# Attention scores in two key halves, and a head spread moved up to stand directly behind them

## The chip, the core and the metric

The kernel runs as one program on one core of a Trainium2 chip. The metric is the device time of one execution in microseconds (us), lower is better. Matrix products run on TensorE (PE in the profile), elementwise work and reductions on VectorE (DVE), exponentials, square roots and copies on ScalarE (ACT), the subtraction that splits the weights on GpSimd (POOL); SyncE (SP) issues the loads of the weights.

## The reference, cut to what matters

Two transformer blocks run one after the other on 512 tokens of width 1024. The change touches three attentions with heads of 64 channels. In the first block that is a causal attention with a bias by distance ("moba" in the kernel). In the even layer of the second block two attentions stand side by side: one over a window of 128 tokens to either side with a sink, and one over a neighbourhood of a grid.

```python
qa = _rmsnorm(qa.reshape(B, S, A_KV_HEADS, A_GROUP, HEAD_DIM), qn_a)
ka = _rmsnorm(ka.reshape(B, S, A_KV_HEADS, HEAD_DIM), kn_a)
oa = _window_gqa(qa, ka, va, sink_a)
qb = _rmsnorm(qb.reshape(B, S, B_HEADS, HEAD_DIM), qn_b)
kb = _rmsnorm(kb.reshape(B, S, B_HEADS, HEAD_DIM), kn_b)
ob = _neighbourhood_attn(qb, kb, vb, rpb_b)
return jnp.concatenate([oa, ob], axis=-1) @ w_out
```

Queries and keys of every head are normalised over their 64 channels (`_rmsnorm`) before the scores. In each attention the score of a query and a key is their product over 64 channels in full float32; bias and mask follow, then a softmax over the keys, then the product with the values.

## The kernel before, in words

Everything is kept feature-major: a block is 128 channels on the partitions and 512 tokens along the free axis. A large product is split into three (high weights with high inputs, high with low, low with high), all of 512 columns; one "unit" is a block of 128 output channels, 8 such triples. The weights come in a ring of four units (`RING`): SP loads a unit, ACT rounds it to its high part, POOL subtracts to get the low part, PE multiplies.

Each engine has its own program, written out by hand in program order, with semaphores between the engines. `pair_attention` (on PE from line 850, on ACT from line 1595, on DVE from line 2277) works through items. An item is one pair of heads and one tile of 128 queries, with 128 to 512 keys. The two heads lie on partitions 0 to 63 and 64 to 127, so each of their score products uses 64 rows of the array; the scores of the two heads go into two banks of `score_ps`. One item goes through these steps:

- PE `scores` (L858): one product for each head over all keys of the item.
- DVE `logits` (L2286): adds the bias and finds the maximum, which frees `score_ps` (semaphore `scores_used`).
- ACT `exps` (L1604, L1607), then DVE `divide` (L2295 to L2299).
- PE `turned` (L867) transposes the probabilities into `turn_ps`, ACT `copies` (L1615) brings them back.
- PE `values` (L882) multiplies by the values into `out_ps`.

The PE loop is skewed: step i holds the scores of item i, the values of item i-3, the transposes of item i-2, and at its end a hook `between(i)` in which the caller places other work. It is a strict order: a wait in the hook holds back all that stands behind it on PE.

The window attention has 16 items, so 19 steps (0 to 18) on PE. Its hook `prepare_neighbour` (L1338 on PE) prepares the neighbour attention beside it. `WINDOW_PIECES` places pieces of the projections (`piece`, L621 to L623). `WINDOW_TURNS` places transposes of values at steps 9, 13 and 17 (L1332). Steps 1 to 8 sum squares per head (L657). Step 10 transposes the norm factors of all 8 blocks into rows (`turn_head_columns`, L664). Then ACT takes the high part of these rows (`high_rows`, L1694) and DVE the low part (`low_rows`, L2178, semaphore `rows_ready`). Steps 11 to 18 each spread one block's factors over its channels (`neighbour_spread`, which is `head_spread`, L670): one product of 64 rows with 512 columns into `gemm_ps[:, 0, :]`. DVE then scales the block by it (`head_scaled`, L2090, semaphore `spread_used`). The first spread waits for `rows_ready`, each later one for `spread_used` of the one before. The neighbour attention follows, with the same helper.

Of the kernel before, what the change touches and what calls it, by code (L numbers as in the profile page):

```python
# [30 lines left out]
P = 128  # L31
# [5 lines left out]
HD = 64  # L37
# [147 lines left out]
def build(nc, x_in, mem_in, w_in, par_in, con_in, moba_in, alibi_in, na_in, dist_in, out):  # L185
    with ExitStack() as ctx:
# [8 lines left out]
        score_ps = ctx.enter_context(nc.psum_tensor("score_ps", [P, 2, N], F32))  # L195
# [133 lines left out]
        def pair_items(kind):  # L329

            items = []
            for b in range(2 if kind == "moba" else 4):
                for t in range(T):
                    lo, hi = (0, t + 1) if kind == "moba" else (max(t - 1, 0), min(t + 2, T))
                    qs, ks = slice(t * P, (t + 1) * P), slice(lo * P, hi * P)
                    it = dict(nk=(hi - lo) * P, tile=t, group=b, last=t == T - 1, first=t == 0, turned=False, sink=None)
                    heads = [slice((2 * b + s) * HD, (2 * b + s + 1) * HD) for s in range(2)]
                    if kind == "moba":
                        it.update(q=proj1[:, A_Q + b, qs], k=proj1[:, A_K + b, ks], to=4 + b,
                                  bias=[moba_bias[:, 2 * b + s, (3 - t) * P:4 * P] for s in range(2)],  # L340
                                  v=[[values_moba[:, c, r] for c in range(lo, hi)] for r in heads])
                    elif kind == "window":
                        it.update(q=proj2[:, E_AQ + b, qs], k=proj2[:, E_AK, ks], to=b,
                                  bias=[alibi[:, 2 * b + s, (lo - t + 1) * P:(hi - t + 1) * P] for s in range(2)],
                                  sink=par[:, PCOL["sink"] + 2 * b:PCOL["sink"] + 2 * b + 2],
                                  v=[[values_a[:, c, s * HD:(s + 1) * HD] for c in range(lo, hi)] for s in range(2)])
                    else:
                        it.update(q=proj2[:, E_BQ + b, qs], k=proj2[:, E_BK + b, ks], to=4 + b, turned=True,
                                  bias=[na_bias[t][:, 2 * b + s, :] for s in range(2)],
                                  v=[[values_b[:, c, r] for c in range(lo, hi)] for r in heads])  # L350
                    items.append(it)
            return items

        def pair_probs(i, s, nk, wide):

            a = (2 * (i % 3) + s) * (N if wide else 3 * P)
            return y_all[:, a:a + nk]
# [211 lines left out]
        def _(pe):  # L569
# [47 lines left out]
            def piece(n, o, first, end, h, l):  # L617

                for kt in range(first, end):
                    w = slice(kt * P, (kt + 1) * P)  # L620
                    pe.matmul(o, wh[:, n % RING, w], h[:, kt, :], start=(kt == 0), stop=False)  # L621
                    pe.matmul(o, wh[:, n % RING, w], l[:, kt, :], start=False, stop=False)
                    m = pe.matmul(o, wl[:, n % RING, w], h[:, kt, :], start=False, stop=(kt == KT - 1))  # L623
                if end == KT:
                    m.then_inc(unit_done, 1)
# [34 lines left out]
            def turn_head_columns(bank):  # L660

                take(head_columns_ready)
                for c in range(T):
                    m = pe.transpose(bank[0:HEAD_ROWS, c * P:(c + 1) * P],  # L664
                                     head_columns[:, c * HEAD_ROWS:(c + 1) * HEAD_ROWS], ident)
                m.then_inc(head_columns_turned, 1)
# [180 lines left out]
                crossed(1, 3, 4).then_inc(unit_done, 1)  # L847
                taken[group_used] = groups0 + 4

            def pair_attention(items, between=lambda i: None, wide=False):  # L850
                groups0 = taken.get(group_used, 0)

                def scores(i, it):
                    if i:
                        take(scores_used)
                    for s in range(2):
                        r = slice(s * HD, (s + 1) * HD)
                        m = pe.matmul(score_ps[:, s, 0:it["nk"]], it["q"][r, :], it["k"][r, :], start=True, stop=True)  # L858
                    m.then_inc(scores_ready, 1)

                def turned(i, it):
                    take(probs_ready)
                    for s in range(2):
                        a = pair_probs(i, s, it["nk"], wide)
                        for c in range(it["nk"] // P):
                            t = slice(c * P, (c + 1) * P)
                            m = pe.transpose(turn_ps[:, s, t], a[:, t], ident)  # L867
                    m.then_inc(probs_turned, 1)

                def values(i, it):  # L870
                    if it["first"] and groups0 + it["group"] >= 2:
                        pe.wait_ge(group_used, groups0 + it["group"] - 1)
                    chunks = it["nk"] // P
                    for c in range(chunks):
                        for s in range(2):
                            o = out_ps[s * HD:(s + 1) * HD, it["group"] % 2, :]
                            if it["turned"]:
                                q = P // 8
                                o = o.rearrange("p (r c) -> p c r", r=8)[:, it["tile"] * q:(it["tile"] + 1) * q, :]
                            else:  # L880
                                o = o[:, it["tile"] * P:(it["tile"] + 1) * P]
                            m = pe.matmul(o, it["v"][s][c], pair_turned[i % 2][:, s, c * P:(c + 1) * P],  # L882
                                          start=(c == 0), stop=(c == chunks - 1))
                    m.then_inc(item_done, 1)

                n = len(items)
                for i in range(n + 3):
                    if i < n:
                        scores(i, items[i])
                    if i >= 3:  # L890
                        take(probs_copied)
                        values(i - 3, items[i - 3])
                    if 2 <= i < n + 2:
                        turned(i - 2, items[i - 2])
                    between(i)
                take(scores_used)
                taken[exp_ready] = taken.get(exp_ready, 0) + n
                taken[group_used] = groups0 + items[-1]["group"] + 1
# [387 lines left out]
            def query_spread(b, bank):  # L1286

                head_spread(b, QUERY_ROWS, bank)
# [14 lines left out]
            for t in range(T):  # L1303
                m = pe.transpose(turn_ps[:, 0, t * P:(t + 1) * P], proj2[:, E_AV, t * P:(t + 1) * P], ident)
# [15 lines left out]
            def neighbour_stat(b):  # L1320

                head_stat(b, y[:, 7 + b % 2, :], gemm_ps[:, 0, :])

            def neighbour_spread(b):

                head_spread(b, NEIGHBOUR_ROWS, gemm_ps[:, 0, :])
# [8 lines left out]
            def prepare_neighbour(i):  # L1335
                if i == 1:
                    take(copied_v)
                    take(spread_used)  # L1338
                if 1 <= i <= 8:
                    neighbour_stat(i - 1)  # L1340
                if i in WINDOW_PIECES:
                    u, first, end = WINDOW_PIECES[i]
                    if first == 0:
                        pe.wait_ge(unit_split, even + u + 1)
                        pe.wait_ge(emptied, even + (7 if u == 8 else u))
                        if u > 14:
                            take(copied_v)
                    piece(even + u, gemm_ps[:, 1, :], first, end, xh, xl)
                if i == 0:
                    pe.wait_ge(emptied, even + 8)  # L1350
                    query_spread(3, gemm_ps[:, 0, :])
                if i in WINDOW_TURNS:
                    turn_neighbour(WINDOW_TURNS[i])
                if i == 10:
                    turn_head_columns(gemm_ps[:, 0, :])
                if i == 11:
                    take(rows_ready)
                if 11 < i <= 18:
                    take(spread_used)
                if 11 <= i <= 18:  # L1360
                    neighbour_spread(SPREAD_ORDER[i - 11])
            pair_attention(pair_items("window"), prepare_neighbour)
            outputs0 = taken[group_used]

            def window_part(i):
# [31 lines left out]
            for kt in range(KT):  # L1397
                m = pe.matmul(o, wl[:, n % RING, kt * P:(kt + 1) * P], xh[:, kt, :], start=False, stop=(kt == KT - 1))
# [1564 lines left out]
```

## Time and profile before

| what | value |
|---|---|
| runs before (3) | 2170.11, 2170.78 and 2171.26 us, median 2170.78 us |
| profiled execution, first to last instruction (span) | 2169.7 us |
| median of the runs less that span | 1.08 us |
| PE busy | 2149.4 us, 99% of the span, 10303 instructions |
| DVE, ACT, POOL busy | 983.0, 847.1 and 893.9 us |
| HBM traffic | 88 GB/s over the span |

The page gives the profiled execution's time as its span; the 1.08 us are what lies around it in a timed run. Busy times are shares over very different stages, and a record of PE includes the depth of the pipeline, so the spacing of starts in the timeline says more than the mean of a record. A float32 product stands in the trace as two records.

### The profile page before, as it was taken

The numbers are of one execution on the slowest core, as the hardware profiler recorded it, in microseconds if no ns is written. First come the engines' busy times: TensorE is split into PE (matmuls) and PEld (weight loads), VectorE is DVE, ScalarE is ACT, GpSimd is POOL, SyncE is SP. The second block draws the span as 40 slices with busy tenths as digits, with TensorE's granted clock in tenths as the row PEclk, the third lists the DMA queues.
The fourth block names the chain that finished last, engine by engine and source line by source line (L and its number), as shares of the span: only waits on it lengthen the run. The fifth ranks groups of instructions, "written<-read, shape, count | busy, mean of one in ns | idle before, by whom it ended". The sixth has DMA issues, their size and how long they took to land.

```text
span 2169.7 us, 27420 instructions
## 1 busy us (share of the span) xinstructions
PE 2149.4 (99%) x10303; PEld 1731.4 (80%) x10303; DVE 983.0 (45%) x1496; ACT 847.1 (39%) x1282; POOL 893.9 (41%) x684
## 2 busy tenths in 40 slices
PE   9999999999999999999999999999999999999999
PEld 7875787788888877767888888888888878888887
DVE  5755645576626143465432231346534655313221
ACT  6435645422222243565433232444333434423221
POOL 5431254154444443213444444433343315444443
PEclk9999999999999999999999999999999999999999
DMA  4222132133322332102222222322222213222223
GB/s 175 78 68 69 57 99 78 59 102 122 106 97 97 110 113 88 50 30 69 97 97 97 97 97 97 106 81 75 78 87 78 72 44 109 97 97 97 97 97 97
DMA packets 55109, 193.24 MB, mean 89 GB/s; under 512 B 6112, under 2 KB 6368, under 8 KB 54752
## 3 DMA queue, kind: packets, MB, share of 16 engines
q1 hardware_dynamic: 50112, 180.41, 25.0%
q10 hardware_dynamic: 4896, 11.41, 1.6%
q8 instruction: 73, 1.20, 0.2%
q14 instruction: 28, 0.23, 0.0%
HBM read 189.69 MB, written 2.10 MB: 88 GB/s over the span
## 4 chain that ended last, share of the span: by engine, by line
issue 52%; POOL 29%; PE 17%; POOLq 1%; DMA 0%; DVE 0%; ACT 0%; SPq 0%; ACTq 0%
POOL wl L552 29%; PE gemm_ps L587 6%; PE gemm_ps L588 6%; PE gemm_ps L589 6%; POOLq L549 0%; POOLq L561 0%; DMA x<-x_in 0%; DVE xl L2090 0%; ACT xh L1892 0%; ACT wh L1497 0%; PE turn_ps L729 0%; DVE x L2236 0%; SPq L526 0%; ACTq L1891 0%
## 5 line engine op out<-in xcount | busy, mean ns | idle before, releaser
L552 POOL TENSOR_TENSOR wl<-raw,wh 128x512 fp32r<-128x512 f32 x678 | 890.1, 1335 | 1258.0 <-ACT wh L1497 1248.8
L1497 ACT ACTIVATE wh<-raw 128x1024 fp32r<-128x1024 f32 x339 | 358.7, 1059 | 752.7 <-DMA raw<-w_in 742.1
L587 PE MATMUL gemm_ps<-xh,wh 128*128 128x512 f32 x1176 | 465.8, 396 | 0.0
L589 PE MATMUL gemm_ps<-xh,wl 128*128 128x512 f32 x1176 | 459.0, 390 | 0.0
L588 PE MATMUL gemm_ps<-xl,wh 128*128 128x512 f32 x1176 | 458.8, 390 | 0.0
L588 PE MATMUL gemm_ps<-arena_r,wh 128*128 128x512 f32 (+1 forms) x1088 | 417.0, 383 | 0.0
L587 PE MATMUL gemm_ps<-arena_r,wh 128*128 128x512 f32 (+1 forms) x832 | 320.0, 385 | 1.2 <-POOL wl L552 0.7
L589 PE MATMUL gemm_ps<-arena_r,wl 128*128 128x512 f32 (+1 forms) x832 | 317.4, 381 | 0.0
L587 PEld LDWEIGHTS gemm_ps<-xh,wh 128*128 128x128 f32 x1176 | 221.5, 188 | 49.6 <-issue 2.3
L588 PEld LDWEIGHTS gemm_ps<-xl,wh 128*128 128x128 f32 x1176 | 221.5, 188 | 47.4 <-issue 2.2
L589 PEld LDWEIGHTS gemm_ps<-xh,wl 128*128 128x128 f32 x1176 | 221.3, 188 | 46.7
L588 PEld LDWEIGHTS gemm_ps<-arena_r,wh 128*128 128x128 f32 x1088 | 205.0, 188 | 41.2 <-issue 1.4
L2090 DVE SCALAR_TENSOR_TENSOR arena<-gemm_ps,rstd 128x512 f32<-128x512 f32 (+1 forms) x116 | 84.7, 731 | 261.9 <-PE gemm_ps L589 211.1
L2236 DVE TENSOR_TENSOR x<-x,gemm_ps 128x512 f32<-128x512 f32 x84 | 57.6, 686 | 316.8 <-PE gemm_ps L589 305.1
L587 PEld LDWEIGHTS gemm_ps<-arena_r,wh 128*128 128x128 f32 x832 | 157.0, 189 | 33.7 <-issue 2.4
L589 PEld LDWEIGHTS gemm_ps<-arena_r,wl 128*128 128x128 f32 x832 | 156.9, 189 | 30.1
L2097 DVE SCALAR_TENSOR_TENSOR tmp<-gemm_ps,rstd 128x512 f32<-128x512 f32 x64 | 44.2, 691 | 207.9 <-PE gemm_ps L589 207.9
L587 PE MATMUL gemm_ps<-y_r,wh 128*128 128x512 f32 x256 | 100.0, 391 | 0.0
L589 PE MATMUL gemm_ps<-y_r,wl 128*128 128x512 f32 x256 | 99.6, 389 | 0.0
L2586 DVE TENSOR_TENSOR arena_r<-sq,arena_r 128x512 fp32r<-128x512 f32 x64 | 93.7, 1464 | 2.2
L621 PE MATMUL gemm_ps<-xh,wh 128*128 128x512 f32 x216 | 88.5, 410 | 1.3 <-DVE xl L2308 0.5
L623 PE MATMUL gemm_ps<-xh,wl 128*128 128x512 f32 x216 | 84.6, 392 | 0.0
(429 smaller groups left out, 2548.6 us busy)
## 6 DMA issues: line engine op xcount, KB each, us to landing
raw<-w_in SPq DMA_DIRECT2D x338, 512.0 KB, 3.4
arena<-na_in ACTq DMA_DIRECT2D x14, 256.0 KB, 2.7
out<-x ACTq DMA_DIRECT2D x8, 256.0 KB, 2.9
x<-x_in SPq DMA_DIRECT2D x6, 256.0 KB, 6.5
arena<-alibi_in ACTq DMA_DIRECT2D x6, 256.0 KB, 3.5
arena<-moba_in ACTq DMA_DIRECT2D x1, 1024.0 KB, 4.8
arena<-mem_in ACTq DMA_DIRECT2D x1, 1024.0 KB, 5.6
arena<-dist_in ACTq DMA_DIRECT2D x1, 896.0 KB, 4.5
```

The lines of the kernel that those rows point to most:

```text
L552: m = pool.tensor_tensor(wl[:, k, half], raw[:, k, half], wh[:, k, half].bitcast(F32), ALU.subtract)
L587: pe.matmul(o, wh[:, n % RING, w], h[:, kt, 0:width], start=(kt == 0), stop=False)
L588: pe.matmul(o, wh[:, n % RING, w], l[:, kt, 0:width], start=False, stop=False)
L589: last = pe.matmul(o, wl[:, n % RING, w], h[:, kt, 0:width], start=False, stop=(kt == nkt - 1))
L621: pe.matmul(o, wh[:, n % RING, w], h[:, kt, :], start=(kt == 0), stop=False)
L623: m = pe.matmul(o, wl[:, n % RING, w], h[:, kt, :], start=False, stop=(kt == KT - 1))
L1497: act.activation(wh[:, k % RING, :], raw[:, k % RING, :], ACT.Copy).then_inc(high_split, 1)
L2090: sent(dve.scalar_tensor_tensor(out=o, in0=a, scalar=scalar, in1=b, op0=op0, op1=op1), s)
L2097: done(dve.scalar_tensor_tensor(out=o, in0=a, scalar=scalar, in1=b, op0=op0, op1=op1), s)
L2236: sent(dve.tensor_tensor(x[:, e, :], x[:, e, :], bank(n0, e), ALU.add), emptied)
L2586: done(dve.tensor_tensor(l[:, b, :], sq[:, b % 2, :], h[:, b, :].bitcast(F32), ALU.subtract), rhs_ready)
```

## The change

Two things change, on PE alone. First, `scores` cuts the keys of an item that has more than 128 of them into two halves and issues head 0 and head 1 of the first half, then head 0 and head 1 of the second. Second, `pair_attention` gets a second hook, `behind_scores(i)`, directly after the scores of step i; the waits and the spread of steps 11 to 18 move from `prepare_neighbour` into it. All three callers (moba, window, neighbour) get the halves, the window call alone the new hook.

```diff
-            def pair_attention(items, between=lambda i: None, wide=False):
+            def pair_attention(items, between=lambda i: None, wide=False, behind_scores=lambda i: None):
                 groups0 = taken.get(group_used, 0)
 
                 def scores(i, it):
                     if i:
                         take(scores_used)
-                    for s in range(2):
-                        r = slice(s * HD, (s + 1) * HD)
-                        m = pe.matmul(score_ps[:, s, 0:it["nk"]], it["q"][r, :], it["k"][r, :], start=True, stop=True)
+                    part = it["nk"] // 2 if it["nk"] > P else P
+                    for k0 in range(0, it["nk"], part):
+                        ks = slice(k0, k0 + part)
+                        for s in range(2):
+                            r = slice(s * HD, (s + 1) * HD)
+                            m = pe.matmul(score_ps[:, s, ks], it["q"][r, :], it["k"][r, ks], start=True, stop=True)
                     m.then_inc(scores_ready, 1)
...
                     if i < n:
                         scores(i, items[i])
+                    behind_scores(i)
                     if i >= 3:
                         take(probs_copied)
                         values(i - 3, items[i - 3])
...
                 if i == 10:
                     turn_head_columns(gemm_ps[:, 0, :])
+
+            def spread_neighbour(i):
                 if i == 11:
                     take(rows_ready)
                 if 11 < i <= 18:
                     take(spread_used)
                 if 11 <= i <= 18:
                     neighbour_spread(SPREAD_ORDER[i - 11])
-            pair_attention(pair_items("window"), prepare_neighbour)
+            pair_attention(pair_items("window"), prepare_neighbour, behind_scores=spread_neighbour)
```

The place on which most rests is PE's program at step 11 of the window attention, from the transposes of the norm factors (`head_columns`) at the end of step 10. `y_r,pair_r` is the first spread. Before, with the nine products of the piece between the last two groups:

```order
L664 MATMUL gemm_ps<-con,head_columns 32x128 x3
L858 MATMUL score_ps<-arena 128x256 [waits scores_used]
L858 MATMUL score_ps<-arena 128x256
L882 MATMUL out_ps<-tmp,arena 64x128 [waits group_used,probs_copied]
L882 MATMUL out_ps<-tmp,arena 64x128 x3
L867 MATMUL turn_ps<-con,y_all 128x128 [waits probs_ready]
L867 MATMUL turn_ps<-con,y_all 128x128 x5
...
L670 MATMUL gemm_ps<-y_r,pair_r 128x512 [waits rows_ready]
L858 MATMUL score_ps<-arena 128x256 [waits scores_used]
```

And now:

```order
L664 MATMUL gemm_ps<-con,head_columns 32x128 x3
L861 MATMUL score_ps<-arena 128x128 [waits scores_used]
L861 MATMUL score_ps<-arena 128x128 x3
L670 MATMUL gemm_ps<-y_r,pair_r 128x512 [waits rows_ready]
L885 MATMUL out_ps<-tmp,arena 64x128 [waits group_used,probs_copied]
L885 MATMUL out_ps<-tmp,arena 64x128 x3
L870 MATMUL turn_ps<-con,y_all 128x128 [waits probs_ready]
L870 MATMUL turn_ps<-con,y_all 128x128 x5
```

The spread and its wait for the factor rows moved up past 4 value products, 6 transposes and the nine products of the piece, and the two score products of 256 columns became four of 128.

The second place is PE's steps 13 and 14, where no piece stands at the end of step 13 but four transposes of values (L1332 before, L1336 now). Before:

```order
L670 MATMUL gemm_ps<-y_r,pair_r 128x512 [waits spread_used]
L858 MATMUL score_ps<-arena 128x384 [waits scores_used]
L858 MATMUL score_ps<-arena 128x384
L882 MATMUL out_ps<-tmp,arena 64x128 [waits probs_copied]
L882 MATMUL out_ps<-tmp,arena 64x128 x5
L867 MATMUL turn_ps<-con,y_all 128x128 [waits probs_ready]
L867 MATMUL turn_ps<-con,y_all 128x128 x3
L1332 MATMUL gemm_ps<-con,arena 128x128 [waits emptied]
L1332 MATMUL gemm_ps<-con,arena 128x128 x3
L670 MATMUL gemm_ps<-y_r,pair_r 128x512 [waits spread_used]
```

And now:

```order
L861 MATMUL score_ps<-arena 128x192 [waits scores_used]
L861 MATMUL score_ps<-arena 128x192 x3
L670 MATMUL gemm_ps<-y_r,pair_r 128x512 [waits spread_used]
L885 MATMUL out_ps<-tmp,arena 64x128 [waits probs_copied]
L885 MATMUL out_ps<-tmp,arena 64x128 x5
L870 MATMUL turn_ps<-con,y_all 128x128 [waits probs_ready]
L870 MATMUL turn_ps<-con,y_all 128x128 x3
L1336 MATMUL gemm_ps<-con,arena 128x128 [waits emptied]
L1336 MATMUL gemm_ps<-con,arena 128x128 x3
L861 MATMUL score_ps<-arena 128x192 [waits scores_used]
```

A spread stood ahead of the scores of the next step and stands behind the scores of its own step now; it still touches a score product on one side.

## Rows read from the trace of the kernel before

**Rows 1.** The page: busy time by engine, share of the span, instructions.

```profile
PE 2149.4 (99%) x10303; PEld 1731.4 (80%) x10303; DVE 983.0 (45%) x1496; ACT 847.1 (39%) x1282; POOL 893.9 (41%) x684
```

**Rows 2.** Timeline of PE, steps 9 to 12: start, length, idle before and releaser.

```profile
909.71 0.92 PE L858 MATMUL score_ps<-arena 64*128 64x384 f32 x4
910.56 0.66 PE L882 MATMUL out_ps<-sq,arena 128*64 128x128 f32 x8
...
914.83 0.70 PE L858 MATMUL score_ps<-arena 64*128 64x256 f32 x4
915.46 0.66 PE L882 MATMUL out_ps<-tmp,arena 128*64 128x128 f32 x8
...
919.31 0.50 PE L670 MATMUL gemm_ps<-y_r,pair_r 64*128 64x512 f32 x1 [0.30 <-DVE y_r L2178]
920.24 0.70 PE L858 MATMUL score_ps<-arena 64*128 64x256 f32 x4 [0.43 <-DVE small L2286]
```

**Rows 3.** Timeline of ACT, then of DVE, up to the factor rows and behind them.

```profile
917.98 0.57 ACT L1694 ACTIVATE y_r<-gemm_ps 32x512 fp32r<-32x512 f32 x1
918.58 0.68 DVE L2178 TENSOR_TENSOR y_r<-gemm_ps,y_r 32x512 fp32r<-32x512 f32 x1 [4.35 <-ACT y_r L1694]
919.29 0.48 DVE L2286 CUSTOM_DVE_ANT_0 y_all<-score_ps,arena,par 128x256 f32<-128x256 f32 x1
921.16 0.74 DVE L2090 SCALAR_TENSOR_TENSOR arena<-arena,par,gemm_ps 128x512 f32<-128x512 f32 x1
```

**Rows 4.** Timeline of PE, steps 13 and 15: a spread beside scores, and one alone.

```profile
923.89 1.13 PE L858 MATMUL score_ps<-arena 64*128 64x384 f32 x4
924.95 0.88 PE L882 MATMUL out_ps<-tmp,arena 128*64 128x128 f32 x12
...
926.78 0.49 PE L670 MATMUL gemm_ps<-y_r,pair_r 64*128 64x512 f32 x1
...
935.82 0.50 PE L670 MATMUL gemm_ps<-y_r,pair_r 64*128 64x512 f32 x1
936.25 0.88 PE L882 MATMUL out_ps<-sq,arena 128*64 128x128 f32 x12
```

**Rows 5.** Timeline of PE: sixteen score records of 128 columns, heads in turn (L1085).

```profile
84.42 1.16 PE L1085 MATMUL score_ps<-tmp 64*128 64x128 f32 x16
85.51 0.50 PE L587 MATMUL gemm_ps<-xh,wh 128*128 128x512 f32 x1
```

**Rows 6.** Timeline of PE: two float32 products of 512 columns on the same rows.

```profile
206.73 1.98 PE L974 MATMUL gemm_ps<-arena,pair_r 32*128 32x512 f32 x4
208.64 0.92 PE L858 MATMUL score_ps<-arena 64*128 64x384 f32 x4
```

**Rows 7.** Stretches, three at the low clock: length, PE busy (x), PEclk, DMA share, GB/s.

```profile
210.78:214.19 3.41, 3.41 (x13) 0.50 0.00 0
214.19:217.60 3.41, 3.41 (x9) 0.50 0.00 0
306.35:309.76 3.41, 3.41 (x17) 0.50 0.14 55
408.75:412.16 3.41, 1.97 (x8) 1.00 0.00 0
```

**Rows 8.** Timeline of PE: spacing at both clocks, before a fall, the longest idle.

```profile
213.10 0.63 PE L589 MATMUL gemm_ps<-xh,wl 128*128 128x512 f32 x1
213.53 0.63 PE L587 MATMUL gemm_ps<-xh,wh 128*128 128x512 f32 x1
...
217.95 0.39 PE L589 MATMUL gemm_ps<-xh,wl 128*128 128x512 f32 x1
218.18 0.39 PE L587 MATMUL gemm_ps<-xh,wh 128*128 128x512 f32 x1
...
304.68 1.05 PE L740 MATMUL turn_ps<-con,sq 128*128 128x4 f32 x8
...
1764.09 0.96 PE L1126 MATMUL score_ps<-arena_r 128*128 128x512 f32 x3 [1.11 <-DVE tmp L2090]
```

## The prediction

> **What bounds the kernel now.** The page comes first: PE is busy 99% of the span, DVE, ACT and POOL under half [rows 1]. So time is won or lost where PE waits, or where its own products get longer or shorter. Next comes PE's timeline in the window attention, read by the spacing of starts. Three things are to be seen. A score item of 384 keys takes 0.85 us to the next group (909.71 to 910.56), one of 256 keys 0.63 us [rows 2]. From the start of the values of step 11 at 915.46 to the first spread at 919.31 PE needs 3.85 us, and only the last 0.30 us of it are idle, waiting for DVE's factor rows [rows 2]. Then the scores of step 12 wait another 0.43 us for DVE. Third come ACT and DVE in the same stretch: ACT begins the high factor rows at 917.98, with no idle time before it, and DVE the low ones at 918.58, ready at about 919.26 [rows 3]. That chain is paced by ACT's own queue, and nothing in it waits for what PE does after 915.46.
>
> **The halves.** Each float32 product leaves two records; an item's four become eight. First the question whether the two heads already run beside each other. Two float32 products of 512 columns on the same rows, one behind the other, take 1.91 us from start to next group (206.73 to 208.64) for four records [rows 6]: at most 0.48 us each, or 0.12 us per record and 128 columns; less something for changing over I put 0.11. An item of 384 keys needs 0.22 us more than one of 256 [rows 2]. Four records of two heads in turn would need four times 0.11, or 0.43 us, for those 128 columns more; two heads at once need two times, or 0.22. So they already run beside each other, and the halves have no overlap left to win.
>
> What they add is pairs of records. Sixteen records of 128 columns, heads in turn, take 1.09 us (84.42 to 85.51) [rows 5]. That is 1024 columns per head in both records together; an item of 256 keys has 512 of these and takes 0.63 us, and another 512 columns in long records cost twice 0.22 us, which makes 1.07. The remaining 0.02 us is the price of six more pairs. Counting the item lists, 18 items have 256 keys, 18 have 384 and 2 have 512; the two with 128 stay whole. 38 items with two more pairs each, at 0.003 to 0.01 us a pair, make 0.2 to 0.8 us, nearly all of it on PE's path; I take +0.3 us. A gain has no row for it except by the rival on order below.
>
> The Trainium skill (TensorE: Matmul & The Clock Gate, Part 3) says that matmuls start and end in strict program order, also across the array's tiles. By that rule head 1 could not start before head 0's second record, an item would have three record slots before and five half slots now; the change would gain, and the sum would be 2170.2 us, the last rival below. The 0.22 us of the trace speak against it here.
>
> **The spreads of steps 12 to 18.** A spread beside scores and the scores together take 1.06 us for 384 keys (923.89 to 924.95), so it adds 0.21 to 0.85; one alone takes 0.43 us (935.82 to 936.25) [rows 4]. Before, four of the seven others touch a score group (behind steps 12, 13, 14 and 18) and three stand alone; now the four of steps 12 to 15 touch one and three stand alone, because steps 16 to 18 have no scores. Sum: 0.
>
> Each now waits for `spread_used` directly behind the scores, with values, transposes and pieces queued behind it. DVE needs from the start of its logits at 919.29 to the end of its scaling at 921.90 some 2.6 us [rows 3], 0.2 to 0.3 more for 384 keys. The shortest step that counts is 13: from its scores' end at 924.95 to the spread at 926.78, plus the next scores of 0.85, makes 2.7 us [rows 2, 4]. That is 0.1 to 0.2 us short at worst, once; I take +0.1 us. In the other direction DVE gets each spread earlier, which wins nothing, since PE doesn't wait for these scalings now.
>
> **The first spread.** This is the large term. Its wait for the factor rows moves from behind 3.55 us of work (3.85 less 0.30) to directly behind the scores, that is from 919.01 to 915.46 [rows 2]. The rows still come at 919.26, so PE stands still for 3.8 us, and the values of item 8, the transposes of item 9, the piece, and the scores of step 12 all queue behind. ACT's copies of item 9 and its exponentials get later too, but PE is what they feed. The new course: spread at 919.31, 0.42 us as one alone, then the 3.55 us of work, so scores of step 12 at 923.28 instead of 920.24. The 0.43 us that those scores waited for DVE is gone and is counted in this. Difference: +3.0 us. Nothing after it absorbs that: DVE and ACT take their work from PE item by item. Bounds: 2.6 us, if the whole of the wait before step 12 comes back as slack later; 3.3 us, if the spread costs more after the standstill.
>
> SP and POOL are not moved past. The unit of that piece is finished 3 us later, so its slot in the ring is refilled 3 us later; POOL, busy 41% [rows 1], covers that.
>
> **The clock.** The trace has stretches in which the granted clock is half: 210.78 to 217.60 and 306.35 to 309.76 among them [rows 7]. There products of 512 columns start every 0.43 us, at the full clock every 0.23 [rows 8]: 1.2 GHz against 2.4. What went before 306.35 was a row of sums of 4 columns [rows 8], hardly any streaming. On the other side, the stretch of 408.75 had PE busy for 1.97 of 3.41 us and kept the clock [rows 7], and so did the longest idle time of the whole trace, 1.11 us at 1764 [rows 8]. A standstill of 3.8 us has no row; it is three times the longest idle, and emptier than what went before 306.35. So I expect the clock to fall in it or behind it. The price of one such stretch, 3.41 us at 0.43 instead of 0.23 us a product, is 3.41 times (1 - 0.23/0.43), or 1.6 us, less where part of the stretch falls into the standstill; of one twice as long 3.2 us. The lower bound is 0. I take 1.6, by the nearest rows.
>
> **Sum.** 0.3 + 0 + 0.1 + 3.0 + 1.6 = +5.0 us on a profiled execution with a span of 2169.7 us and 1.08 us around it to the median of the runs, 2170.78. Predicted: **2175.8 us**. A measurement of this kernel can tell about 0.2%, or 4.3 us, from no change, so the sum lies a little beyond that.
>
> **The rivals.**
> - The clock does not fall, or only inside the standstill. For it: the idle time of 1.11 us left the clock alone. Against it: the falls that are there came with less. The sum without 1.6 gives +3.4 us, 2174.2 us, which is no measurable change.
> - The clock falls for two stretches, as at 210.78 [rows 7]. For it: behind the standstill come transposes and short groups as there. +6.6 us, 2177.4 us.
> - No standstill forms: the factor rows are ready by 915.5. The place is ACT's queue before 917.98; it would have to run 3.8 us ahead. Against it: no idle time in front of the row [rows 3]. What is left is +0.4 us, 2171.2 us.
> - The other side: strict order holds between the heads after all. Then the halves save, per item, three record slots less five of half the length, since only neighbouring records of different heads could overlap. With 0.107 us per 128 columns (0.43 / 4) that is 3 x 0.32 - 5 x 0.16 = 0.16 us for 384 keys, 0.11 for 256, 0.21 for 512, together 18 x 0.16 + 18 x 0.11 + 2 x 0.21 = 5.3 us. Against the 4.7 us of wait and clock that is 2170.2 us, and 2168.6 without the fall. It decides if an item of 384 keys gets shorter than 0.85 us; the growth of 0.22 us speaks against it.
>
> **How the numbers follow.** Chances: forecast 0.44, no fall 0.25, two stretches 0.17, no standstill 0.09, strict order 0.05. The first three share the standstill, at 0.86; the clock splits them. The range 2173.0 to 2177.8 us runs from the case without a fall with its low bound (3.0 - 0.4, nothing for halves or step 14, less 0.4 for the runs' own spread) to two stretches with the high bound of the halves (0.7 of it on the path, 3.0 + 0.7 + 0.1 + 3.2 = 7.0); outside stay the last two cases. Slower by over 0.2% is the forecast except for its lowest part (0.40) and two stretches (0.17), 0.57; within 0.2% is no fall, no standstill, most of the strict order and that lowest part, 0.40; faster 0.03.
>
> **What would show it.** In the trace after, the first spread (L670) should carry an idle time of some 3.8 us released by DVE L2178, with the values of step 11 (L885) behind it; the scores of step 12 should follow the first spread by some 4.0 us instead of 0.93. The 384-key scores should still take about 0.85 us to the next group where no spread is beside them. The stretch behind the standstill should show PEclk 0.50 once, for about 3.4 us. The prediction is wrong if the first spread waits under 1 us, if the score groups get shorter by a tenth of a microsecond or more, or if PE's idle times in the neighbour attention shrink by what the standstill cost.

## The result, and the profile after

The changed kernel takes 2185.37 us (median of 6 runs, 2181.78 to 2188.17), the kernel before 2170.76 us beside it (6 runs, 2167.70 to 2173.11). The ratio is 1.0073 with a 95% interval of 1.0063 to 1.0083: 0.7% slower, some 14.6 us. Forecast were 2175.8 us and at most 2177.8. The direction was right, the size a third of what came.

First the page of the changed kernel, busy time by engine, and the stretches around its low clock in the window attention (length, PE busy, PEclk, DMA share, GB/s):

```profile
PE 2160.7 (99%) x10455; PEld 1750.0 (80%) x10455; DVE 983.5 (45%) x1496; ACT 847.2 (39%) x1282; POOL 893.6 (41%) x684
```

```profile
921.05:927.87 6.82, 6.76 (x24) 0.50 0.01 2
948.35:951.77 3.42, 3.42 (x11) 0.50 0.00 0
955.18:962.01 6.83, 6.83 (x24) 0.50 0.00 0
```

The profiled execution took 2187.88 us with a span of 2185.9 us. PE is busy 11.3 us more than before [rows 1], DVE, ACT and POOL are as they were. Busy time grew because PE ran at half clock more often: three such stretches, 17.1 us together, lie where the kernel before had none. Outside the change, too, this execution has 10.2 us more of it (a stretch of 6.8 us at 405, and the one at 781 twice as long), but there the span grew by 0.9 us only, as the next rows show.

Now PE's timeline of the changed kernel, from the scores of step 11 to the spread of step 18 (start, length, line, idle before and what released it; from step 13 on the spreads alone; rows 2 and 4 show these groups before), and at its end the scores of item 4 of the neighbour attention:

```profile
916.63 0.72 PE L861 MATMUL score_ps<-arena 64*128 64x128 f32 x8
921.11 0.79 PE L670 MATMUL gemm_ps<-y_r,pair_r 64*128 64x512 f32 x1 [3.76 <-DVE y_r L2184]
921.83 1.12 PE L885 MATMUL out_ps<-tmp,arena 128*64 128x128 f32 x8
...
928.07 0.71 PE L861 MATMUL score_ps<-arena 64*128 64x128 f32 x8
928.54 0.48 PE L670 MATMUL gemm_ps<-y_r,pair_r 64*128 64x512 f32 x1
...
933.82 0.49 PE L670 MATMUL gemm_ps<-y_r,pair_r 64*128 64x512 f32 x1 [0.95 <-DVE arena L2096]
936.70 0.52 PE L670 MATMUL gemm_ps<-y_r,pair_r 64*128 64x512 f32 x1
941.25 0.47 PE L670 MATMUL gemm_ps<-y_r,pair_r 64*128 64x512 f32 x1
946.75 0.49 PE L670 MATMUL gemm_ps<-y_r,pair_r 64*128 64x512 f32 x1 [1.55 <-DVE arena L2096]
953.51 0.49 PE L670 MATMUL gemm_ps<-y_r,pair_r 64*128 64x512 f32 x1 [1.73 <-DVE arena L2096]
956.27 0.79 PE L670 MATMUL gemm_ps<-y_r,pair_r 64*128 64x512 f32 x1
...
971.93 0.71 PE L861 MATMUL score_ps<-arena 64*128 64x128 f32 x8 [0.46 <-DVE small L2292]
```

The first spread stands still for 3.76 us on DVE's factor rows, as forecast (3.8). But the spreads of steps 13, 16 and 17 wait too, for 0.95, 1.55 and 1.73 us on DVE's scaling (L2096), and the forecast had 0.1 us there. From 916.63 to 971.93 are 55.30 us. The kernel before has the same two marks at 914.83 [rows 2] and, in this row of its own timeline, at 954.83, 40.00 us:

```profile
954.83 0.70 PE L858 MATMUL score_ps<-arena 64*128 64x256 f32 x4 [0.47 <-DVE small L2286]
```

So 15.3 us of the spans' difference of 16.2 us arise between these two marks. This distance is called **the stretch** below. It leaves out the clock of other stages, which differs from run to run and which the medians carry as well; but it comes from one profiled execution of each kernel, and that need not be a typical one.

A ledger of the 15.3 us: idle time 3.76 + 0.95 + 1.55 + 1.73 = 8.0 us, less the 0.73 us that were idle at this place before [rows 2], makes 7.3. The half clock costs 17.1 us times (1 - 0.23/0.43), the price from rows 8, or 7.9. Sum 15.2.

What held DVE back is in its own timeline of the changed kernel. L2096 with `rstd` scales a finished projection, with `par` it scales by a spread; L2311 is the marker of a finished output group.

```profile
932.12 1.08 DVE L2096 SCALAR_TENSOR_TENSOR arena<-gemm_ps,rstd 128x512 f32<-128x512 f32 x1 [1.47 <-PE gemm_ps L623]
933.05 0.71 DVE L2096 SCALAR_TENSOR_TENSOR arena<-arena,par,gemm_ps 128x512 f32<-128x512 f32 x1
...
945.86 0.06 DVE L2311 MEMSET eps<- 128x1 f32 x1 [2.36 <-ACT y_all L1627]
945.95 0.75 DVE L2096 SCALAR_TENSOR_TENSOR arena<-arena,par,gemm_ps 128x512 f32<-128x512 f32 x1
...
951.82 1.08 DVE L2096 SCALAR_TENSOR_TENSOR arena<-gemm_ps,rstd 128x512 f32<-128x512 f32 x1 [4.20 <-PE gemm_ps L623]
952.74 0.72 DVE L2096 SCALAR_TENSOR_TENSOR arena<-arena,par,gemm_ps 128x512 f32<-128x512 f32 x1
```

In steps 12 and 16 DVE's program puts the scaling of the projection whose last piece PE computes in the same step ahead of the scaling by the spread. The latter ends at 933.8 and 953.5, and there PE goes on (933.82, 953.51). In step 15 it is the finished output group: DVE waits 2.36 us for ACT's copy of it (L1627) before it scales, and PE goes on at 946.75.

### The profile page after: what moved, and what is told of

It reads as the page before. It is cut to its first block, busy times and chain, and to the rows that moved or that the text cites. A ratio compares the mean times of both kernels' runs of the same rounds, so it can differ in the third digit from the quotient of the medians.

```text
span 2185.9 us, 27724 instructions
## 1 busy us (share of the span) xinstructions
PE 2160.7 (99%) x10455; PEld 1750.0 (80%) x10455; DVE 983.5 (45%) x1496; ACT 847.2 (39%) x1282; POOL 893.6 (41%) x684
## 4 chain that ended last, share of the span: by engine, by line
issue 53%; POOL 29%; PE 17%; POOLq 1%; DMA 0%; DVE 0%; ACT 0%; SPq 0%; ACTq 0%
POOL wl L552 29%; PE gemm_ps L587 6%; PE gemm_ps L588 6%; PE gemm_ps L589 6%; POOLq L549 0%; POOLq L561 0%; DMA x<-x_in 0%; DVE xl L2096 0%; ACT xh L1898 0%; ACT wh L1503 0%; PE turn_ps L729 0%; DVE x L2242 0%; SPq L526 0%; ACTq L1897 0%
## 5 line engine op out<-in xcount | busy, mean ns | idle before, releaser
L2096 DVE SCALAR_TENSOR_TENSOR arena<-gemm_ps,rstd 128x512 f32<-128x512 f32 (+1 forms) x116 | 84.7, 732 | 267.1 <-PE gemm_ps L589 212.1
```

Of the source, the lines that this page charges most:

```text
L2096: sent(dve.scalar_tensor_tensor(out=o, in0=a, scalar=scalar, in1=b, op0=op0, op1=op1), s)
```

## The experiments

Theory W: the loss is the waits of the moved spreads, the first on the factor rows and three on DVE's order, and the half clock behind them; the halves cost nothing. The "stretch" is given against 40.00 us of the kernel before. The kernel before was run beside each on the same chip.

**1. The halves alone** (`e1`): the first hunk of the diff without the rest.

> The kernel before with the score products in halves and nothing else. Theory W (the whole loss comes from the moved spreads' waits and from the clock that falls in and behind them): 2170.8 + 0.0 to 0.8 us, no measurable change; a 384-key score group still takes about 0.85 us to the next group. Rival H (the halves cost: 152 more records of PE): +3 us or more, spread over the three attentions. Rival O (strict order, the halves gain): -3 to -5 us, and the 384-key groups come down to about 0.7 us.

2170.11 us, ratio 1.0003 (0.9994 to 1.0012), stretch +0.05 us. A 384-key group takes 0.85 us to the next (906.39 to 907.24), as before:

```profile
906.39 0.92 PE L861 MATMUL score_ps<-arena 64*128 64x192 f32 x8
907.24 0.66 PE L885 MATMUL out_ps<-sq,arena 128*64 128x128 f32 x8
```

By themselves the halves show neither a cost nor a gain. Rival O, strict order between the heads, is out, and so is Rival H's cost of 3 us or more for the 152 records: the interval ends at 2.6 us.

**2. The spreads alone** (`e2`): the changed kernel with the old `scores`.

> The changed kernel with whole score products, so the moved spreads alone. Theory W: within 1.5 us of the changed kernel, 2184 to 2187 us, with the same idle times in front of the spreads of steps 11, 13, 16 and 17 (3.8, 1.0, 1.6 and 1.7 us) and stretches at half clock behind them. Rival H: at least 3 us less than the changed kernel.

2179.68 us, ratio 1.0050 (1.0037 to 1.0064), stretch +13.77. The waits are those of the changed kernel to 0.02 us (3.78, 0.96, 1.55, 1.73). Low clock: 13.7 us. The total misses theory W's 2184 to 2187 us: it lies 5.7 us under the changed kernel's first median, which Rival H would have. The profiled execution was the slowest of the five (2185.04 us). Runs 12 and 13 go into this.

**3. The first spread back at the end of step 11** (`e3`).

```diff
+                if i == 11:
+                    take(rows_ready)
+                    neighbour_spread(SPREAD_ORDER[0])
 
             def spread_neighbour(i):
-                if i == 11:
-                    take(rows_ready)
                 if 11 < i <= 18:
                     take(spread_used)
-                if 11 <= i <= 18:
                     neighbour_spread(SPREAD_ORDER[i - 11])
```

> The changed kernel, but the first spread (step 11) stays at the end of its step; those of steps 12 to 18 stand behind the scores. Theory W: no standstill of 3.8 us and no fall behind it; the waits of steps 13, 16 and 17 stay, 4.2 us in sum, with one or two stretches at half clock behind 16 and 17 (3.4 to 10.2 us at 0.23/0.43 of the rate, 1.6 to 4.7 us): 2175 to 2180 us. Rival F (the first standstill alone makes the loss, and the later waits are its echo): 2171 to 2172 us.

2180.30 us, ratio 1.0046 (1.0033 to 1.0060), stretch +12.17. The standstill is gone, and yet most of the loss stays: waits of 0.95, 1.56 and 1.73 us, and a new one of 1.00 us in step 12, since the first spread is now so late that its scaling isn't done when the next wants the bank:

```profile
921.21 0.49 PE L670 MATMUL gemm_ps<-y_r,pair_r 64*128 64x512 f32 x1 [1.00 <-DVE arena L2097]
```

Stretches at half clock follow here too (922, 942 and 949; 13.7 us). Rival F is out. The upper end of the expectation was passed by 0.3 us.

**4. Only the first spread moved** (`e4`): the mirror of run 3, steps 12 to 18 keep their place.

> The changed kernel, but only the first spread stands behind the scores (step 11); those of steps 12 to 18 stay at the end of their steps. Theory W: the standstill costs 3.0 us net and a fall of 3.4 or 6.8 us behind it 1.6 or 3.2 us: 2175 to 2177.5 us; the later waits are gone. Rival F: close to the changed kernel, 2183 us or more. Rival C (the falls come by chance and not from the waits): 2174 us, with no low stretch right behind the standstill.

2173.98 us, ratio 1.0021 (1.0012 to 1.0031), stretch +4.56. The total is 1.0 us below theory W's 2175 to 2177.5. One standstill, one fall, no other wait:

```profile
915.24 0.50 PE L670 MATMUL gemm_ps<-y_r,pair_r 64*128 64x512 f32 x1 [3.76 <-DVE y_r L2185]
```

```profile
916.10:919.51 3.41, 3.41 (x17) 0.50 0.02 5
919.51:960.00 40.49, 39.88 (x307) 1.00 0.12 40
```

That is the forecast's own mechanism: it had 3.0 + 1.6 = 4.6 us for this part. The median is the 2174 us of Rival C; the low stretch right behind the standstill speaks against that rival.

**5. Products into the standstill** (`e5`).

```diff
                 if i == 11:
+                    pe.wait_ge(probs_copied, taken[probs_copied] + 1)
+                    for n in range(8):
+                        pe.matmul(turn_ps[:, n % 2, :], ident, con[:, 0:N], start=True, stop=True)
                     take(rows_ready)
```

> The changed kernel with eight float32 products of 512 columns (about 0.43 us each) into the idle transpose banks ahead of the wait for the factor rows, results unused. PE is as late as before but not idle. Theory W (the standstill itself makes the clock fall): no stretch at half clock right behind 920; from the first value product on the time is 1.6 to 3.2 us less than in the changed kernel, the three later waits and their falls stay: 2181 to 2184 us. Rival C (the fall comes from what stands behind, short and half-empty groups, or by chance): a low stretch of 3.4 or 6.8 us stays there.

2182.97 us, ratio 1.0051 (1.0035 to 1.0067), stretch +15.57.

```profile
917.47 7.13 PE L1365 MATMUL turn_ps<-con 128*128 128x512 f32 x16
```

```profile
914.00:948.50 34.50, 31.72 (x199) 1.00 0.05 17
```

The clock keeps its full rate up to 948.5, so the fall behind 920 comes from the standstill itself. But the time hardly moved: the eight products lasted 7.1 us instead of 3.4, since one leaves two records of 0.43 us. The later waits and falls stayed. The total is inside the expectation, for a reason that it didn't have.

**6. DVE scales by the spread first** (`e6`).

```diff
                     if 1 <= i <= n:
                         divide(i - 1, items[i - 1])
+                    early(i)
                     late = 4 if i >= n - 1 or items[0]["nk"] == P else 5
...
-                if 11 <= i <= 18:
+            def scale_neighbour(i):
+                if 11 <= i <= 18:
                     b = SPREAD_ORDER[i - 11]
...
-            pair_attention(pair_items("window"), prepare_neighbour, whole=True)
+            pair_attention(pair_items("window"), prepare_neighbour, whole=True, early=scale_neighbour)
```

> The changed kernel; on DVE the scaling by the spread stands directly behind the divisions of its step, ahead of the outputs and of the scaling of the finished projection. Theory W (the waits of steps 13, 16 and 17 come from DVE's order: its scaling stands behind work that waits for PE's own step): these waits fall from 4.2 us to under 0.5 us in sum and the low stretches behind 16 and 17 vanish; the standstill of 3.8 us and its fall stay: 4.5 to 6.5 us over the kernel before, 2174 to 2176.5 us. Rival L (PE comes late to them in any case, the order is not it): waits of over 3 us stay, 2180 us or more.

2174.49 us, ratio 1.0015 (1.0005 to 1.0025), stretch +4.61. All three later waits are gone, and with them every low stretch behind 924 (the spreads of steps 11, 13, 16 and 17):

```profile
919.53 0.49 PE L670 MATMUL gemm_ps<-y_r,pair_r 64*128 64x512 f32 x1 [3.75 <-DVE y_r L2184]
...
929.51 0.53 PE L670 MATMUL gemm_ps<-y_r,pair_r 64*128 64x512 f32 x1
...
940.84 0.50 PE L670 MATMUL gemm_ps<-y_r,pair_r 64*128 64x512 f32 x1
944.27 0.49 PE L670 MATMUL gemm_ps<-y_r,pair_r 64*128 64x512 f32 x1
```

```profile
920.76:924.17 3.41, 3.41 (x12) 0.50 0.02 5
924.17:960.00 35.83, 35.27 (x265) 1.00 0.13 45
```

Rival L is out: it was DVE's order.

**7. Both, with eight products** (`e7`: edits 5 and 6).

> Both edits together: eight products in the standstill and DVE's scaling moved up. Theory W: only the lateness of 3.0 us is left, without any low stretch between 900 and 1000: 2.8 to 3.8 us over the kernel before, 2172.5 to 2174.5 us. Rival: over 5 us, then something else is in the loss.

2176.18 us, ratio 1.0024 (1.0015 to 1.0033), stretch +6.30. This misses theory W's 2172.5 to 2174.5 us and lies where the rival had it, over 5 us above the kernel before. There is no low stretch, as theory W has it, but the eight products end some 3.3 us after the rows are ready. Run 10 repeats the test with four, and the stretch is 3.3 us shorter there.

**8. The factor rows earlier as well** (`e8`): edit 6, and on ACT `high_rows` of step 10 ahead of `exps` instead of behind.

```diff
                     if 2 <= i < n + 2:
                         copies(i - 2, items[i - 2])
+                    early(i)
                     if i < n:
                         exps(i, items[i])
...
-                if i == 10:
-                    high_rows(NEIGHBOUR_ROWS, gemm_ps[:, 0, :])
...
+            def rows_early(i):
+                if i == 10:
+                    high_rows(NEIGHBOUR_ROWS, gemm_ps[:, 0, :])
```

> The changed kernel with DVE's scaling moved up, and on ACT the high factor rows ahead of the exponentials of step 10 instead of behind them. Theory W: the rows are ready about 3 us sooner (near 916.4 on the time base of the kernel before), the standstill shrinks to about 1 us and makes no fall: within 1 us of the kernel before, no measurable change. Rival: the exponentials that are now 0.6 us later hold back the transposes, and 2 us or more stay.

2169.49 us, ratio 0.9992 (0.9983 to 1.0000), stretch +0.03. The standstill is 0.76 us and nothing falls:

```profile
918.44 0.49 PE L670 MATMUL gemm_ps<-y_r,pair_r 64*128 64x512 f32 x1 [0.76 <-DVE y_r L2187]
```

```profile
914.00:960.00 46.00, 44.38 (x332) 1.00 0.11 36
```

The whole loss is gone with both edits of the change still in. They are harmless once the spreads' producers are early enough, and they win nothing: run 9, with the same edit on ACT in the old order of PE, has a stretch 1.1 us shorter.

**9. The kernel before with the rows early** (`e9`): the ACT edit of run 8 alone.

> The kernel before (whole score products, spreads at the end of their steps), with one edit: ACT makes the high factor rows ahead of the exponentials of step 10. Theory W: the idle times of 0.30 and 0.43 us around the first spread vanish and nothing else changes: 0.5 to 0.9 us less in the stretch, too little to be told from no change in the total. Rival: the exponentials 0.6 us later hold the transposes back and the stretch gets longer.

2169.18 us, ratio 0.9994 (0.9985 to 1.0003), stretch -1.10 us. Both idle times of rows 2 are gone. This is the shortest stretch of all, by more than expected, but the total can't be told from no change.

**10. Four products and DVE's order** (`e10`: run 7 with 4 in place of 8).

> As the run with eight products and DVE's scaling moved up, but with four products: a float32 product of 512 columns takes two records of 0.43 us, so eight lasted 7.1 us and made PE 3 us later than the factor rows did. Four last about 3.5 us and end before the rows come. Theory W: the stretch from 910 to 960 is 2.8 to 3.6 us longer than in the kernel before, with no low stretch in it. Rival: it stays 4.5 us or more longer, then something besides the fall is lost with the standstill.

2173.65 us, ratio 1.0017 (1.0008 to 1.0026), stretch +3.04. PE waits just as long but isn't idle, and the clock stays up:

```profile
916.14 3.70 PE L1365 MATMUL turn_ps<-con 128*128 128x512 f32 x8
919.96 0.49 PE L670 MATMUL gemm_ps<-y_r,pair_r 64*128 64x512 f32 x1
```

```profile
914.00:960.00 46.00, 45.33 (x327) 1.00 0.11 35
```

Against run 6 (+4.61) the difference is 1.57 us: the price of one stretch of 3.41 us at half clock, which the forecast had at 1.6. What remains, 3.04, is the lateness that it had at 3.0.

**11. DVE scales by the spread ahead of the projection only** (`e11`): in DVE's hook the two blocks change places; the output group stays ahead.

> The changed kernel; on DVE the scaling by the spread goes ahead of the scaling of the finished projection, but stays behind the outputs of a finished group. Theory W: the waits of steps 13 and 17 (0.95 and 1.73 us) vanish, that of step 16 (1.55 us, behind the outputs that wait for ACT) stays; one low stretch behind it at most: 2174 to 2178 us. Rival L: all three stay or all three vanish.

2176.51 us, ratio 1.0027 (1.0017 to 1.0037), stretch +6.27. Exactly the two waits behind a projection vanish, the one behind the output group stays (the spreads of steps 13, 15, 16 and 17):

```profile
929.64 0.53 PE L670 MATMUL gemm_ps<-y_r,pair_r 64*128 64x512 f32 x1
...
937.09 0.47 PE L670 MATMUL gemm_ps<-y_r,pair_r 64*128 64x512 f32 x1
942.60 0.49 PE L670 MATMUL gemm_ps<-y_r,pair_r 64*128 64x512 f32 x1 [1.55 <-DVE arena L2096]
946.02 0.49 PE L670 MATMUL gemm_ps<-y_r,pair_r 64*128 64x512 f32 x1
```

Against run 6 the stretch is longer by 1.66 us, the wait and nearly nothing else, and no low stretch follows it here:

```profile
924.34:960.00 35.66, 34.11 (x254) 1.00 0.10 32
```

**12 and 13. The changed kernel and the spreads alone, side by side.**

> The changed kernel itself, beside the moved spreads alone on the same chip. Theory W: 12 to 16 us over the kernel before, and within 1.5 us of the moved spreads alone: what differs between the two earlier results (1.0073 and 1.0050) is the length of the stretches at half clock. Rival H2 (the halves make these stretches longer, though they cost nothing without them): again 3 to 5 us over the moved spreads alone, and in its profile more time at half clock between 915 and 965.

> The moved spreads alone (whole score products) once more, as the partner of the run above. Theory W: 12 to 16 us over the kernel before. Rival H2: 9 to 11 us.

2182.30 us, ratio 1.0061 (1.0045 to 1.0077), and 2179.87 us, ratio 1.0048 (1.0032 to 1.0064). Over the kernel before (2170.71 us) that is 11.6 and 9.2 us. Both are less than theory W had, and the second lies in Rival H2's 9 to 11; the medians differ by 2.4 us, between the two expectations, and the intervals overlap. In the profiles it is the other way round: the changed kernel has the shorter stretch (+12.34 against +13.79) and less half clock in it (10.2 us against 13.7). But its profiled execution was the fastest of the six (2178.74 us). Its waits are those of the first profile to 0.02 us:

```profile
914.87 0.49 PE L670 MATMUL gemm_ps<-y_r,pair_r 64*128 64x512 f32 x1 [3.75 <-DVE y_r L2184]
...
945.80 0.49 PE L670 MATMUL gemm_ps<-y_r,pair_r 64*128 64x512 f32 x1 [1.73 <-DVE arena L2096]
```

```profile
915.80:919.21 3.41, 3.41 (x15) 0.50 0.02 5
939.69:943.10 3.41, 3.41 (x21) 0.50 0.02 5
946.52:949.93 3.41, 3.41 (x21) 0.50 0.11 43
```

So one and the same kernel lost 15.3 us in this stretch in one profile and 12.3 in another, and the 3.0 us between them go with 6.9 us of half clock.

Whether the halves make the clock fall more where the waits are stays open. The 12 executions with halves (the first result and run 12) took on average 13.6 us more than the mean of the kernel before beside them, the 11 without (runs 2 and 13) 11.0. The difference of 2.6 us has a 95% interval of about 0 to 5 us, and the mean granted clock is 0.9933 with the halves and 0.9953 without. The profiles, one of each run, can't tell. In run 8, which has the halves but hardly a wait, no loss is left.

## Why the prediction was wrong

- **The halves: right by themselves.** +0.3 us was forecast, the stretch of run 1 shows +0.05, its total no change that can be told. That the two heads already ran beside each other, read from the 0.22 us between 256 and 384 keys, fits run 1: a group of 384 keys takes 0.85 us whole and in halves. What the halves do to the clock behind the waits is open. The Trainium skill (TensorE: Matmul & The Clock Gate, Part 3) states that matmuls start and end in strict program order. Read record by record, as the forecast's last rival reads it, that would have made these groups shorter, and run 1 does not bear this reading out.
- **The first spread: right.** Standstill 3.76 us against 3.8, lateness 3.04 (run 10) against 3.0.
- **The clock behind it: right for one stretch.** 1.57 us (run 10 against run 6) against 1.6. Whether it stays low for 3.4 or 6.8 us differs between executions; the forecast had both as cases.
- **The spreads of steps 12 to 18: here it failed.** The step was: "DVE needs from the start of its logits at 919.29 to the end of its scaling at 921.90 some 2.6 us", applied to all steps, with the outcome "0.1 to 0.2 us short at worst, once". Rows 3 show step 11, in which nothing stands between the divisions and the scaling. In steps 12 and 16 the scaling of a projection stands there, which waits for PE's last piece of the same step; in step 15 the output group, which waits for ACT. Before the change these waits of DVE were covered, because PE asked for the scaling only at the end of its next step. The three waits measured 4.2 us instead of 0.1. The kernel before already showed them, in its own timelines of DVE and PE:

```profile
924.99 0.71 DVE L2090 SCALAR_TENSOR_TENSOR arena<-arena,par,gemm_ps 128x512 f32<-128x512 f32 x1
936.64 0.75 DVE L2090 SCALAR_TENSOR_TENSOR arena<-arena,par,gemm_ps 128x512 f32<-128x512 f32 x1
940.30 0.71 DVE L2090 SCALAR_TENSOR_TENSOR arena<-arena,par,gemm_ps 128x512 f32<-128x512 f32 x1
939.25 0.49 PE L670 MATMUL gemm_ps<-y_r,pair_r 64*128 64x512 f32 x1
```

The scalings of steps 12, 15 and 16 ended there at 925.70, 937.39 and 941.01. In the new order PE asks for them at the end of the scores of step 13 (923.89 [rows 4] and 0.85 us), where the spread of step 15 stood (935.82 [rows 4]) and where that of step 16 stood (939.25). That is 0.96, 1.57 and 1.76 us too early; 0.95, 1.55 and 1.73 came. In the same way the 921.90 of step 11, against scores that end at 920.24 + 0.63, gives 1.03 us for the wait of step 12 in run 3, which was 1.00.

- **The clock behind those waits** was not in the sum at all, since the waits were priced at 0.1 us. In every profile that had both waits (the changed kernel twice, runs 2, 3, 5 and 13) the clock fell behind step 16's and again behind step 17's, for 6.8 to 10.2 us together, or 3.2 to 4.8 us of time.

Together: 3.0 + 1.6 was forecast for the first spread and 0.1 for the others; the others cost 7.8 to 9.2 us (12.34 in run 12 and 13.77 in run 2, each less run 4's 4.56; the 15.3 of the first profile has 1.6 more for a first fall twice as long). The range ended at 2177.8 because its case of longest half clock still had only one place where PE waits. None of the signs that the forecast had named for being wrong came: it had named none for the spreads of steps 12 to 18.

## What to carry to other kernels

When a wait moves up in an engine's program, read the producer's program for every step in which the wait occurs, not for one: what stands ahead of the signal there, and whether it waits for work that the waiting engine now does later. Here the timeline before the change held the answer: when the producer ended in each step, set against the place where the consumer was going to stand. A delay that was hidden by slack becomes a wait as soon as that slack is gone. And price an idle time on PE with the clock that it may cost: here the half clock cost 4.8 to 7.9 us beside 7.3 us of waits.

## What the runs showed of the hardware

- The clock fell behind idle time much shorter than the 3.8 us that the forecast was about. A low stretch began 0.7 to 1.6 us behind the wait of 1.55 us in step 16 in six of the seven profiles that have this wait, and a second one behind the 1.73 us of step 17 in the same six. Run 11, in which the waits of steps 13 and 17 are gone, has the wait of 1.55 us without a fall. In run 3 a fall came 0.8 us behind a wait of 1.00 us, while the wait of 1.11 us of rows 8 had none. What decides it, these runs don't settle.
- How long it stays low is not the kernel's alone: the same program, with the same waits to 0.02 us, spent 17.1 us of this stretch at half clock in one execution and 10.2 in another. The kernel before ranged from 2165.9 to 2173.8 us over all runs beside these experiments, and low stretches elsewhere come and go as well: its profile has them at 211, 306 and 781 us, that of run 1 at 401 and 776. A difference of a few us between two executions can be that alone, so the stretch between two marks helps to place it.
- PE kept busy in the standstill with products that nobody reads kept the clock there (runs 5, 7 and 10). A float32 product of 512 columns takes two records of 0.43 us each at the full clock.
